# Sparse-attention decode stage: compression rows laid out contiguously, page numbers kept in registers, score and value products in column tiles of 64

## The reference, cut to what matters

```python
def compress(x, pos, w1, b1, w2):            # once for keys, once for values
    ch = x[:, :n_ch * 16].reshape(b, n_ch, 16, 2, 128)
    blocks = concatenate([ch[:, :-1], ch[:, 1:]], axis=2) + pos   # 127 blocks of 32 rows, 16 rows apart
    h = silu(einsum('bnlgd,lde->bnge', blocks, w1) + b1)
    return einsum('bnge,ed->bngd', h, w2)

past = cache_c_kv[page_table]                 # (8, 2048, 4, 2, 128): k_cmp, v_cmp, k_slc, v_slc
# per query: attention over the 127 compressed rows; those scores choose 16 blocks of 64 tokens;
# attention over the chosen blocks (k_slc, v_slc); attention over a window of 512; three gated outputs summed
s_s = einsum('bqghd,bgqkld->bgqhkl', q, k_sel) * scale + bias
o_s = einsum('bgqhkl,bgqkld->bqghd', softmax(s_s), v_sel)
```

## Time and profile before

| | |
|---|---|
| Median of three runs | 3275.92 us (3275.68 to 3283.25) |
| Profiled execution, own time | 3270.58 us |
| Its span, first to last instruction | 3268.9 us |
| TensorE matmul busy in the span | 2742.4 us (84%) |
| VectorE, ScalarE, GpSimd busy | 40%, 22%, 4% |
| Mean granted TensorE clock | 0.894 of 2.4 GHz |
| Phase `block_sample_c`, first DMA issue to the last sequence's result | about 1935 to 2922 us |

### The profile page before, as it was taken

One profiled execution on the slowest core, in us unless ns is written; L12 is line 12 of the kernel. 1 busy time (PEld: TensorE's weight loads), 2 busy tenths in 40 slices (PEclk: granted clock), 3 DMA queues, 4 the chain that ended last, 5 costly groups with the idle time before them and its releaser, 6 DMA issues. The chain is left out here.

```text
span 3268.9 us, 49787 instructions
## 1 busy us (share of the span) xinstructions
PE 2742.4 (84%) x18609; PEld 2328.9 (71%) x18609; DVE 1302.6 (40%) x2405; ACT 733.8 (22%) x1077; POOL 138.2 (4%) x308
## 2 busy tenths in 40 slices
PE   6999998899947886677898954888998899879787
PEld 3999998889935765577898953456555665557587
DVE  3336996445612333445234610123222321225644
ACT  2333333323402221122133310011111110112331
POOL 1000000000040000000000030000000000000000
PEclk7999999999968998789798985999998999886889
DMA  5566897537889996384387667355435544513272
GB/s 160 184 203 222 313 331 259 199 123 282 300 280 377 398 395 241 106 296 167 139 304 267 213 175 268 114 192 184 157 121 187 184 142 135 188 66 111 85 256 78
DMA packets 260298, 686.66 MB, mean 210 GB/s; under 512 B 31781, under 2 KB 83789, under 8 KB 256523
## 3 DMA queue, kind: packets, MB, share of 16 engines
q1 hardware_dynamic: 216428, 420.10, 37.8%
q0 software_dynamic: 17312, 229.03, 19.6%
q10 hardware_dynamic: 26400, 35.46, 2.9%
HBM read 631.32 MB, written 250.80 MB: 270 GB/s over the span
## 5 line engine op out<-in xcount | busy, mean ns | idle before, releaser
L392 DVE TENSOR_TENSOR w_lo<-w,w_hi 128x2048 fp32r<-128x2048 f32 x180 | 412.7, 2301 | 422.8 <-ACT w_hi L333 401.5
L304 PE MATMUL zb<-xh,w_hi 128*128 128x320 f32 x1664 | 494.5, 310 | 33.0 <-ACT w_hi L329 20.7
L333 ACT CAST w_hi<-w 128x2048 fp32r<-128x2048 f32 x176 | 335.5, 1908 | 728.2 <-PE zb L304 220.3
L304 PE MATMUL zb<-xT_lo,w_hi 128*128 128x320 f32 x1664 | 492.6, 310 | 0.0
L304 PEld LDWEIGHTS zb<-xh,w_hi 128*128 128x128 f32 x1664 | 315.4, 190 | 34.3 <-ACT w_hi L329 20.8
L304 PEld LDWEIGHTS zb<-xT_lo,w_hi 128*128 128x128 f32 x1664 | 313.9, 189 | 0.2
L310 PE MATMUL zb<-xh,w_lo 128*128 128x320 f32 x1664 | 265.3, 311 | 17.0 <-DVE w_lo L392 17.0
L310 PEld LDWEIGHTS zb<-xh,w_lo 128*128 128x128 f32 x1664 | 252.1, 190 | 18.0 <-DVE w_lo L392 18.0
L304 PE MATMUL zc<-xh,w_hi 128*128 128x320 f32 x704 | 211.0, 314 | 22.3 <-ACT w_hi L333 15.1
L1796 PE MATMUL hb<-xtc,cmp_w 128*128 128x254 f32 x512 | 221.3, 606 | 6.7 <-issue 3.3
L1796 PE MATMUL m<-xtc,cmp_w 128*128 128x254 f32 x512 | 220.6, 605 | 0.0
(11 more groups left out here) (351 smaller groups left out, 3825.5 us busy)
## 6 DMA issues: line engine op xcount, KB each, us to landing
out<-in_cache_a_kv POOLq DMA_DIRECT2D x32, 4080.0 KB, 17.2
w<-in_w_in_even SPq DMA_DIRECT2D x104, 1024.0 KB, 6.0
ka<-in_cache_a_kv SPq DMA_DIRECT2D x24, 2048.0 KB, 19.9
va<-in_cache_a_kv SPq DMA_DIRECT2D x24, 2048.0 KB, 19.5
w<-in_w_in_odd SPq DMA_DIRECT2D x44, 1024.0 KB, 6.2
raw<-in_cache_c_kv SPq DMA_DIRECT2D x128, 256.0 KB, 2.6
sel<-in_cache_c_kv SPq DMA_DIRECT2D x128, 256.0 KB, 2.6
out<-in_cache_a_kv POOLq DMA_DIRECT2D x8, 4032.0 KB, 15.3
```

The costliest lines, as they stand in the source:

```text
L304: ins = pe.matmul(self.banks[c][:, 0:T], self.hi[:, q % 2, j, c * P:(c + 1) * P], x[:, q * self.kq + j, :], start=(q == 0 and j == 0 and m ...
L333: act.copy(self.hi[:, q % 2, :, :], self.wt[:, q % 4, :, :]).then_inc(self.hi_ready, 1)
L392: dve.tensor_tensor(self.lo[:, q, :, :], self.wt[:, q, :, :], self.hi[:, q % 2, :, :], ALU.subtract).then_inc(self.lo_ready, 1)
```

## The change

Three edits in `block_sample_c`:

- `xtc` becomes four-dimensional: row within a stride of 16 first, stride number last. The copy out of PSUM does the reordering, and the compression matmuls read runs of 127 neighbouring values.
- The whole page table is loaded once into one partition of SBUF (`pt`); at the start of each sequence's loads 16 page numbers go from there to registers, which serve the `raw` and the `sel` pages.
- Score products: each group has its own 64 columns of weights and writes its own 64 PSUM rows, without adding up. Value products: each group multiplies its own 64 columns of `pttc` with its own 128 columns of values; twice the number of matmuls at half the width.

```diff
-        xt = k.sb("xtc", [P, 4, PAST])
+        pt = k.sb("pt", [1, NB * NPG], I32)
+        xt = k.sb("xtc", [P, 4, CS, PAST // CS])
...
+                sp.dma_start(pt[:, :], k.page_table.rearrange("b n -> (b n)").unsqueeze(0)).then_inc(pt_in, 16)
                 cmp.sync(sp)
...
+                sp.wait_ge(pt_in, 16)
+
                 def load(b, first=False):
+                    _, numbers = nc.values_load_multi_w_load_instructions(
+                        pt[0:1, bass.ds(b * NPG, NPG)], engines=[mybir.EngineType.SP], min_val=0, max_val=k.cache_c_kv.shape[0] - 1)
...
-                            page = sp.value_load(k.page_table[bass.ds(b, 1), pg:pg + 1], min_val=0, max_val=k.cache_c_kv.shape[0] - 1)
-                            sp.dma_start(dst[:, pg, :], k.cache_c_kv[bass.ds(page, 1)].rearrange("a t c g d -> (a t) (c g d)")[:, lo:hi]
+                            sp.dma_start(dst[:, pg, :], k.cache_c_kv[bass.ds(numbers[pg], 1)].rearrange("a t c g d -> (a t) (c g d)")[:, lo:hi]
...
-                    copy(xt[:, :, q * P:(q + 1) * P], bank[:, :].rearrange("p (c n) -> p c n", c=4)).then_inc(sem, 1)
+                    nq = P // CS
+                    copy(xt[:, :, :, q * nq:(q + 1) * nq], bank[:, :].rearrange("p (c n l) -> p c l n", c=4, l=CS)).then_inc(sem, 1)
...
-                            ins = pe.matmul(sb_[fill % 2][:, o:o + P], qc[:, g, :], ktt[:, q % 2, 2 * j + g, :], start=(g == 0), stop=(g == CG - 1))
+                            rows = slice(g * 64, (g + 1) * 64)
+                            ins = pe.matmul(sb_[fill % 2][rows, o:o + P], qc[:, g, rows], ktt[:, q % 2, 2 * j + g, :], start=True, stop=True)
...
                     if n == 5:
                         pe.wait_ge(vn_in, b * 32 + 32)
+                        settle(pe, k)
                     for j in range(4 if n < 5 else 2):
-                        if n == 0:
-                            w, v = ptt[:, q % 2, j, :], win[:, j, CKV:2 * CKV]
...
-                            ins = pe.matmul(hb[:, 0:CKV], w, v, start=(n == 1 and j == 0), stop=(n == 5))
+                        for g in range(CG):
+                            rows, cols = slice(g * 64, (g + 1) * 64), slice(CKV + g * HD, CKV + (g + 1) * HD)
+                            if n == 0:
+                                w, v = ptt[:, q % 2, j, rows], win[:, j, cols]
...
+                                ins = pe.matmul(hb[rows, g * HD:(g + 1) * HD], w, v, start=(n == 1 and j == 0), stop=(n == 5))
...
-                                            xt[:, 2 * i:2 * i + 2, l:l + CS * (NCS - 1) + 1:CS], start=(l == 0), stop=(l == CB - 1))
+                                            xt[:, 2 * i:2 * i + 2, l % CS, n0:n0 + NCS], start=(l == 0), stop=(l == CB - 1))
```

More of the change, by code:

```diff
@@ L1773, in values @@
                         pe.wait_ge(vn_in, b * 32 + 32)
+                        settle(pe, k)
                     for j in range(4 if n < 5 else 2):
-                        if n == 0:
-                            w, v = ptt[:, q % 2, j, :], win[:, j, CKV:2 * CKV]
[L1777 to L1783, removed]
-                            ins = pe.matmul(hb[:, 0:CKV], w, v, start=(n == 1 and j == 0), stop=(n == 5))
+                        for g in range(CG):
+                            rows, cols = slice(g * 64, (g + 1) * 64), slice(CKV + g * HD, CKV + (g + 1) * HD)
+                            if n == 0:
+                                w, v = ptt[:, q % 2, j, rows], win[:, j, cols]
+                            elif n < 5:
+                                w, v = ptt[:, q % 2, j, rows], sel[:, (n - 1) * 4 + j, cols]
+                            else:
+                                w, v = ptt[0:NQ, q % 2, j, rows], vn[:, j, g * HD:(g + 1) * HD]
+                            if n == 0 or (n, j) == (5, 1):
+                                ins = pe.matmul(ob[rows, cols], w, v, start=(n == 0 and j == 0), stop=(n == 5))
+                            else:
+                                ins = pe.matmul(hb[rows, g * HD:(g + 1) * HD], w, v, start=(n == 1 and j == 0), stop=(n == 5))
                     ins.then_inc(pv_q, 1)
@@ L1795, in one @@
                         for l in range(CB):
+                            n0 = l // CS
                             ins = pe.matmul((hb, m2)[i][:, 0:CG * NCS], cmp.w1[:, i, l, :],
-                                            xt[:, 2 * i:2 * i + 2, l:l + CS * (NCS - 1) + 1:CS], start=(l == 0), stop=(l == CB - 1))
+                                            xt[:, 2 * i:2 * i + 2, l % CS, n0:n0 + NCS], start=(l == 0), stop=(l == CB - 1))
                         ins.then_inc(h_done, 1)
```

## The result

| | before | after |
|---|---|---|
| Median | 3279.59 us (3275.68 to 3285.91, 4 runs) | 2987.43 us (2978.59 to 2992.0, 4 runs) |
| Profiled execution, own time | 3270.58 us | 2988.08 us |
| Its span | 3268.9 us | 2986.5 us |

The ratio is 0.9104 with a 95% interval of 0.9077 to 0.9132. The forecast was 2977 us in a range of 2950 to 3040.

A forecast was written before the change was run, and what follows sets the result against it. TensorE's own stream was taken as the bound, compression its largest part. Gains of 221 + 28 + 15 + 12 + 23 - 0.5 = 299 us from 3270.6 gave 2972, with 5.3 for the median 2977 us; range 2950 to 3040.

The forecast's parts named there:

- A: Compression matmuls: contiguous rows save 0.216 us on each of 64 records a half, 221 us over 8 sequences.
- B: SyncE's page loads: numbers in registers gain 28 us in sequence 0's turn stage and 15 us in other sequences' waits.
- C: Score products: column tiles gain 1.5 us a sequence, 12 us in all, ends 0 and 19.
- D: Value products: column tiles gain 2.9 us a sequence, 23 us in all, ends 5 and 30.
- table load: Page table's load, one issue ahead of the compression weights, for which TensorE waits anyway: 0.5 us lost.
- The price in the copy: Copy out of PSUM, now reading every 16th value and writing runs of 8: taken as zero extra time.
- The rival of slow copies: Copies out of PSUM slow down because the source hops at each value: 44 us lost, 3021 us; chance 0.09.
- SyncE would be the bound: SyncE's queue: with compression halved and page loads unchanged, its some 95 us a sequence would set the pace.
- the rival of draining: TensorE's array drains at each of 256 width changes, 0.28 us and not 0.11: 44 us lost, 3021 us; chance 0.04.
- The DMA rival: DMA engines set the pace, at 65% usable time a period of 83 us: 64 us lost, 3041 us; chance 0.08.
- slower: Width changes stall TensorE over 1.17 us each, so the gain is gone; at 1.5 us, 3361 us; chance 0.02.

The follow-up runs named there:

- A alone: Contiguous compression rows as the only change to the kernel before, without page numbers in registers or column tiles: 3249.65 us, ratio 0.9917.

## Why the prediction was right, and where its sizes were off

The sum was 299 us; the spans of the two profiled executions differ by 3268.9 - 2986.5 = 282.4. Term by term, from the profiles:

| term | forecast, us | measured, us | how |
|---|---|---|---|
| A | 221 | 219 | 16 x (27.45 - 13.78) |
| B, sequence 0 | 28 | 31.8 | 44.98 - 13.18 |
| B, other waits for `raw` | 15 | 15.6 | none left |
| C and D | 12 + 23 | 36 | what remains of the sequences' 270.6 |
| table load | -0.5 | -9.4 | 59.34 - 68.79 |
| phase starts and ends later | 0 | -10.6 | below |

The row of C and D: seven periods became shorter by 766.6 - 526.8 = 239.8 us (last copies at 2155.01 and 2921.65 us before), and sequence 0 behind its turn by 30.8. Less A and the 15.6 that is 36. It takes up what the other rows leave, and is good to some 8 us: the kernel before with only the table's load added has periods of 108.36 us instead of 109.52. The medians of the runs gave 24 for both tile forms, the periods 32. The last row is no part of the change. The wait for weights began at 1938.55 us instead of 1929.65, and in the control, the same kernel once more, at 1931.2; over all profiled kernels, with and without the change, it began between 1924.3 and 1943.2. 1.7 us lie behind the phase.

- **A** was right to 1%, and 220.5 us by the runs with registers. That the stride is the cause, and that the odd start and the two runs cost nothing, is now shown: 13.78 us with the runs of 127, 14.53 and 28.79 with the same matmuls at strides of two and four.
- **The price in the copy** was rightly taken as zero: 691 and 586 ns for a copy out of PSUM that reads every 16th value. The rival of slow copies is gone. The Trainium skill's 1.73 ns for a column whose source hops at every element (Vector Engine (DVE) Microarchitecture Reference, section 5.2, Measured stream behaviour on trn2), measured there on SBUF and with hops of 4 KiB, would have added some 0.35 us to each, an estimate. On this source, PSUM, with hops of 64 bytes, the trace shows none of it.
- **B**: right, and in sequence 0 better by 4 us than I dared to say. But the forecast's "SyncE would be the bound" at some 95 us was too mild: the round took 111 us, which is why A alone gave 26 us and hardly any of the tiles' gain showed without registers.
- **C**: a score step with its transposes takes 2230.61 - 2229.44 = 1.17 us. The kernel before has 1.33:

```profile
2227.16 1.06 PE L1765 MATMUL scb<-kttc,qc 128*128 128x128 f32 x8
...
2228.49 1.06 PE L1765 MATMUL scb<-kttc,qc 128*128 128x128 f32 x8
```

  0.16 us gained instead of 0.24. The tile records take 0.59 us up to the next transposes, of which 4 x 0.11 is their work: a change of width costs 0.15 us. The forecast's 0.11 is a misreading of the earlier trace rows. In that loop the products of the values follow those of the scores (L981) directly, in tiles of 32 too:

```profile
1034.40 0.62 PE L1009 MATMUL ops<-va,pz 128*32 128x128 f32 x16
```

  So its 0.34 us cover two changes and not three, 0.17 each, and tiles of 32 and of 64 cost about the same. By the periods the scores gave 6 to 11 us for the 12 forecast.
- **D**: a step with its transposes fell from 2.16 us (2255.40 - 2253.24 in the profile before) to 2256.03 - 2254.41 = 1.62, and the first after the softmax from 3.65 to 1.74. By the periods 21 to 26 us for the 23 forecast. Against the 0.11 in the sum, 0.15 us makes 256 x 0.04 = 10 us for the rival of draining, where it had 44. The Trainium skill (TensorEngine Tiling (Array Packing), section Key Properties) says that a change of the mode drains the TensorE. If that means that the next record waits for the end of the last, it costs 0.28 - 0.11 = 0.17 us, an estimate from the earlier trace rows, and the trace's 0.15 agrees roughly. So the rule may hold and the rival's price of 0.28 was too high; the runs don't settle it.
- **The table's load** is the term that failed: "one issue ahead of the compression weights [...] 0.5 us lost". It counted the issue (0.26 us) and not what the load does to the transfers behind it, and "for which TensorE waits anyway" is no cover: the wait grows by the delay, and the pages of sequence 0 come later by it too. In the profiled pair that is 9 of the 16.6 us between 299 and 282.4; the later start and end make 10.6, and the other terms came out some 3 us better than forecast. By the medians of the result the gain is 292 us and 7 are missing. Why so small a load holds up the weights stays open: moving it behind them won back 4 to 6 us of the 8, and the rest wasn't found.
- **The DMA rival** didn't come: the share is 0.68 in a sequence at a period of 76 us, without a wait for pages.
- **A slip in a rival**: "slower" leaves out the 0.11 us a change that the sum already held. The gain would be gone at 1.28 us a change and not at 1.17, and 1.5 us would give 3333 and not 3361.

## What to carry to other kernels

Where a TensorE operand is float32 and strided in SBUF, compare the spacing of its records with that of a contiguous one at the same clock; here two values on 16 bytes kept 95% of the speed and one value halved it, and the reordering was free in the copy out of PSUM. Before adding up gains on one engine, take a full round of every queue that feeds it, gaps and loop cost included: here two bounds stood level at 108 to 111 us, and an edit to TensorE's work alone gave a tenth or less of what it gave once the other bound was lifted (26 of 221 us; of the tiles' 24 us 2, which is no gain clear of noise). A load put ahead of something that is waited for is charged by that wait, not by its own issue.

## What the runs showed of the hardware that I had not expected

- The loss by stride is a step between 8 and 16 bytes: 13.78, 14.53, 28.79 and 27.45 us for half a compression at strides of 1, 2, 4 and 16 values. That 16 is 5% faster than 4 is unexplained.
- At TensorE's lower clock the stride of 16 costs next to nothing. In the kernel before, with the clock at 0.50 (1.2 GHz) from 2496.96 to 2500.00 us, seven records take 3.04 us, 0.43 each, as at 2.4 GHz. With contiguous rows alone, at 0.50 from 2162.4 to 2167.0 us, eleven take 4.6 us, 0.42 each, against 0.215 at 2.4 GHz. Both stretches stand behind a turn stage in which TensorE waited for pages. So, as far as these rows go, contiguous rows gain only where the higher clock is granted.
- A 512-byte load into one partition, issued first, delays 128-partition loads behind it by some 8 us (59.3 to 67.2), four such loads by hardly more (70.8, where nine kernels with one have 65.1 to 70.3).
- SyncE's loads of a page number from memory are slower beside heavy transfers: 16 `raw` pages take 60 us to issue, 16 `sel` pages 39, with the same instructions. In the round shown the DMA engines were busy 0.60 and 0.32 of the two stretches, and the longest load of a pointer took 7.1 and 1.4 us. That the transfers are the cause was not tried.
